# A one-core hybrid layer with routed experts: small loads on ScalarE's queue, tables in strips, later bias loads, unread products

## The reference, cut to what matters

```python
h = h + hybrid_mixer(rms_norm(h, norm1_gain), w_in, ...)   # ends in concat([h_m, h_g]) @ w_out
hn = rms_norm(h, norm2_gain)
logits = hn @ w_router + b_router                           # 512 x 32
top_logit, top_idx = lax.top_k(logits, 4); gate = softmax(top_logit)
# for each expert e, the tokens that chose it, in blocks:
hb = xb @ w_up[e] + b_up[e]                                  # 1024 -> 2048
act = min(glu, 7) * sigmoid(1.702 * min(glu, 7)) * (clip(lin, -7, 7) + 1)
y  += (act @ w_down[e] + b_down[e]) * gate
out = rms_norm(h + y, final_gain)
```

## Time and profile before

| what | value |
|---|---|
| median of three runs | 1299.21 us |
| profiled execution | 1301.6 us, its span 1298.9 us |
| TensorE busy | 1131.2 us, 87% of the span |
| chain that ended last | DMA 58%, PE 30%, SPq 6%, DVE 3% |
| HBM traffic | 447.43 MB read, 25.04 MB written, 364 GB/s over the span |
| mixer and first tiles | up to some 273 us |
| routing | some 273 to 301 us |
| experts | some 301 to 1257 us |
| sums and final norm | to 1298.9 us |

### The profile page before, as it was taken

One profiled execution on the slowest core, in us unless ns is written; L12 is line 12 of the kernel. 1 busy time (PEld: TensorE's weight loads), 2 busy tenths in 40 slices (PEclk: granted clock), 3 DMA queues, 4 the chain that ended last, 5 costly groups with the idle time before them and its releaser, 6 DMA issues.

```text
span 1298.9 us, 28681 instructions
## 1 busy us (share of the span) xinstructions
PE 1131.2 (87%) x11031; PEld 519.3 (40%) x11032; DVE 496.7 (38%) x1245; ACT 201.7 (16%) x293; POOL 217.6 (17%) x384
## 2 busy tenths in 40 slices
PE   8999999989989998989989898989797989797750
PEld 4445554534434443434444333434343434343320
DVE  1393453564423432423343332323233323232317
ACT  2104321111111111111111111111111111111101
POOL 1000112001212221212221111212121212121112
PEclk9999999989979999989999999999899999999995
DMA  9308307668999999999999999999999999999997
GB/s 352 119 33 280 109 1 300 242 234 341 419 422 405 412 425 427 425 426 427 424 426 426 423 425 425 424 425 424 422 426 426 424 427 422 422 426 424 425 419 278
DMA packets 67945, 472.84 MB, mean 364 GB/s; under 512 B 9072, under 2 KB 27052, under 8 KB 42704
## 3 DMA queue, kind: packets, MB, share of 16 engines
q1 hardware_dynamic: 57928, 447.29, 83.4%
q0 software_dynamic: 7776, 20.46, 4.1%
q10 hardware_dynamic: 2216, 4.75, 1.0%
HBM read 447.43 MB, written 25.04 MB: 364 GB/s over the span
## 4 chain that ended last, share of the span: by engine, by line
DMA 58%; PE 30%; SPq 6%; DVE 3%; issue 3%; ACT 0%; POOL 0%; POOLq 0%; DVEq 0%; ACTq 0%
DMA W<-in_w_up_dram 55%; PE B L1271 11%; PE B L1569 8%; PE B L1423 3%; PE B L1586 3%; PE B L1302 2%; SPq L314 2%; SPq L319 1%; SPq L397 1%; DMA W<-in_b_router_dram 1%; SPq L399 1%; DMA hres<-misc,idx_s 1%; DVE W L1233 1%; DMA W<-in_w_in_dram 0%; DVE W L1234 0%
## 5 line engine op out<-in xcount | busy, mean ns | idle before, releaser
L1569 PE MATMUL B<-W,misc 128*32 128x512 f32 x4992 | 593.4, 622 | 114.7 <-DMA W<-in_w_up_dram 90.4
L1569 PEld LDWEIGHTS B<-W,misc 128*32 128x32 f32 x4992 | 186.0, 113 | 469.9 <-issue 463.8
L1586 PE MATMUL B<-W,misc 128*32 128x256 f32 x4992 | 286.8, 380 | 1.1 <-DVE misc L1178 0.9
L1586 PEld LDWEIGHTS B<-W,misc 128*32 128x32 f32 x4992 | 191.3, 111 | 119.0 <-issue 50.0
L1158 DVE TENSOR_TENSOR misc<-B,misc 128x512 f32<-128x512 f32 x78 | 54.0, 692 | 409.0 <-PE B L1569 408.3
L696 ACT ACTIVATE misc<-misc 128x256 f32<-128x256 f32 x78 | 32.5, 416 | 821.1 <-DVE misc L1162 821.1
L1271 PE MATMUL B<-W 128*128 128x512 f32 x320 | 140.2, 593 | 0.0
L513 POOL COPY idx_g<-idx_tab 128x1 uint32 (+1 forms) x77 | 14.3, 185 | 583.3 <-DVE misc L1192 559.2
L696 ACT ACT_TABLE_LOAD x78 | 100.1, 1283 | 9.3 <-DVE idx_tab L1141 7.9
L525 POOL DMA_INDIRECT yrow<-misc,idx_s x75 | 75.1, 1002 | 135.0 <-DVE misc L1180 135.0
L1271 PEld LDWEIGHTS B<-W 128*128 128x128 f32 x320 | 59.6, 190 | 69.1 <-issue 69.1
(11 more groups left out here) (294 smaller groups left out, 514.9 us busy)
## 6 DMA issues: line engine op xcount, KB each, us to landing
W<-in_w_up_dram SPq DMA_DIRECT2D x128, 2048.0 KB, 13.3
W<-in_w_down_dram SPq DMA_DIRECT2D x64, 2048.0 KB, 9.8
W<-in_w_in_dram SPq DMA_DIRECT2D x5, 2048.0 KB, 19.8
yrow<-W SPq DMA_DIRECT2D x1, 8192.0 KB, 40.9
W<-yrow SPq DMA_DIRECT2D x4, 2048.0 KB, 19.9
W<-in_x_dram SPq DMA_DIRECT2D x8, 512.0 KB, 6.8
W<-in_w_out_dram SPq DMA_DIRECT2D x1, 4096.0 KB, 15.7
W<-in_w_in_dram SPq DMA_DIRECT2D x2, 1024.0 KB, 7.0
```

The lines of the kernel that those rows point to most:

```text
L1569: ins = mm(B[0][BT * j:BT * (j + 1), :].rearrange("p (g h c) -> p g h c", g=2, h=2), xT[:, BT * k:BT * (k + 1)], up(par)[:, k, :, :, P * j ...
L1586: ins = mm(B[5][BT * j:BT * (j + 1), 0:QC], aT[:, BT * q:BT * (q + 1)], down(par)[:, q, QC * j:QC * (j + 1)], start=(q == 0), stop=(q == N ...
```

## The change

Four edits. (1) The four small loads are issued by ScalarE, on its queue, after `squares_gating` of tile 3 and ahead of `squares_h(0)`, under the same three waits, in the order `wr`, `rb`, two gain rows. SP keeps the three waits. TensorE's wait for them moves from `router_turn(0)` to `router_strips(0)`. (2) `table` writes its 16 products to four strips of 32 partitions in turn; the small tables and the spreading matrices get 128 partitions, and `spread_table` sums over 128 rows instead of 32. (3) The up-bias row is loaded ahead of piece 3 instead of piece 1, the down-bias row behind piece 5 instead of ahead of piece 4, each with its wait. (4) `busy(n)` makes n products of 128 rows and 128 columns that nothing reads; ten of them stand ahead of four waits in the routing stage.

```diff
 # SP
-            for n in range(2):
-                sp.dma_start(n2row[n], norm2_gain[...].broadcast_to([P, 512])).then_inc(s_n2row, 16)
-            sp.dma_start(wr, w_router[0].rearrange("(k p) n -> p k n", p=P)).then_inc(s_n2row, 16)
-            sp.dma_start(rb, b_router.broadcast_to([P, NE])).then_inc(s_n2row, 16)
...
-                        if n == 1:
+                        if n == 3:
                             sp.wait_ge(m_z, done)
                             load_bias_up(sp, par, e)
-                        if n == 4:
-                            sp.wait_ge(m_ys, done)
-                            load_bias_dn(sp, par, e)
                         if n >= AHEAD:
                             sp.wait_ge(s_w[par][n - AHEAD], 16 * i + 16)
                         load_piece(sp, par, n, e)
+                    sp.wait_ge(m_ys, done)
+                    load_bias_dn(sp, par, e)
 # ScalarE, between squares_gating(3) and squares_h(0)
+            act.wait_ge(s_p, NT * H)
+            act.wait_ge(s_hm, NT)
+            act.wait_ge(s_hgr, NT)
+            act.dma_start(wr, ...).then_inc(s_n2row, 16)
+            act.dma_start(rb, ...).then_inc(s_n2row, 16)
+            for n in range(2):
+                act.dma_start(n2row[n], ...).then_inc(s_n2row, 16)
 # VectorE
-                V.tensor_copy(spread16, ident[0:BT, 0:BT]...)
-                V.tensor_copy(spread, ident[0:BT, 0:BT]...)
+                V.tensor_copy(spread16, fold32.unsqueeze(1).broadcast_to([P, H, BT]))
+                V.tensor_copy(spread, fold32.unsqueeze(1).broadcast_to([P, H, BT]))
-            V.tensor_copy(tok_s, B[5][0:BT, 0:NBMAX])
+            V.tensor_copy(tok_s, B[5][:, 0:NBMAX])
-                V.tensor_copy(gate_s, B[1][0:BT, 0:NBMAX])
+                V.tensor_copy(gate_s, B[1][:, 0:NBMAX])
 # TensorE
 router_turn:
-                else:
-                    pe.wait_ge(s_n2row, 64)
 router_strips:
+                if c == 0:
+                    pe.wait_ge(s_n2row, 64)
 table:
-                    ins = mm(B[bank][0:BT, 0:NBMAX], U[:, a, :], G[:, a, :], start=(a == 0), stop=(a == NT * TOPK - 1))
+                    s = a % 4
+                    ins = mm(B[bank][BT * s:BT * (s + 1), 0:NBMAX], U[:, a, :], G[:, a, :], start=(a < 4), stop=(a >= 12))
...
+            def busy(n):
+                for _ in range(n):
+                    mm(B[4][:, 0:128], ident[:], wr[:, 0:4, :], start=True, stop=True)
             pe.wait_ge(s_pick, 1)
             pick_rows(0, range(NT - 1))
+            busy(2)
             pe.wait_ge(s_mk, NT)
...
+            busy(3)
             pe.wait_ge(s_pick, 2)
             pick_rows(0, range(NT - 1, NT)).then_inc(s_picked, 1)
+            busy(1)
             late_rows()
+            busy(4)
             place_ranks()
```

More of the change, by code:

```diff
@@ L226, in hybrid_layer @@
         lo16, hi16 = r(8).bitcast(f16), r(8).bitcast(f16)
-        tok_s, gate_s = r(48).bitcast(f16)[0:BT, :], r(96)[0:BT, :]
-        spread16 = r(64).bitcast(f16)[0:BT, :].rearrange("p (j t) -> p j t", j=H)
-        spread = r(128)[0:BT, :].rearrange("p (j t) -> p j t", j=H)
+        tok_s, gate_s = r(48).bitcast(f16), r(96)
+        spread16 = r(64).bitcast(f16).rearrange("p (j t) -> p j t", j=H)
+        spread = r(128).rearrange("p (j t) -> p j t", j=H)
         G32 = R[:, 14360:15896].rearrange("p (a g) -> p a g", a=16)
@@ L367, in _ @@
             sp.wait_ge(s_hgr, NT)
-            for n in range(2):
-                sp.dma_start(n2row[n], norm2_gain[:, 512 * n:512 * (n + 1)].broadcast_to([P, 512])).then_inc(s_n2row, 16)
-            sp.dma_start(wr, w_router[0].rearrange("(k p) n -> p k n", p=P)).then_inc(s_n2row, 16)
-            sp.dma_start(rb, b_router.broadcast_to([P, NE])).then_inc(s_n2row, 16)
             first(1, 1)
@@ L406, in _ @@
                             load_bias_up(sp, par, e)
-                        if n == 4:
-                            sp.wait_ge(m_ys, done)
-                            sp.nop(nofuse=True)
-                            load_bias_dn(sp, par, e)
                         if n >= AHEAD:
@@ L413, in _ @@
                         load_piece(sp, par, n, e)
+                    sp.wait_ge(m_ys, done)
+                    sp.nop(nofuse=True)
+                    load_bias_dn(sp, par, e)
             done = sp.value_load(base_tab[0:1, NE - 1:NE], min_val=NE - 1, max_val=NBMAX - 2)
@@ L683, in _ @@
                             (gelu_vg, 2), (squares_vg, 2), (squares_gating, 0), (gelu_u, 2), (squares_gating, 1),
-                            (gelu_vg, 3), (squares_vg, 3), (squares_gating, 2), (gelu_u, 3), (squares_gating, 3),
-                            (squares_h, 0), (squares_h, 1), (squares_h, 2), (squares_h, 3)):
+                            (gelu_vg, 3), (squares_vg, 3), (squares_gating, 2), (gelu_u, 3), (squares_gating, 3)):
                 step(c)
+            act.wait_ge(s_p, NT * H)
+            act.wait_ge(s_hm, NT)
+            act.wait_ge(s_hgr, NT)
+            act.dma_start(wr, w_router[0].rearrange("(k p) n -> p k n", p=P)).then_inc(s_n2row, 16)
+            act.dma_start(rb, b_router.broadcast_to([P, NE])).then_inc(s_n2row, 16)
+            for n in range(2):
+                act.dma_start(n2row[n], norm2_gain[:, 512 * n:512 * (n + 1)].broadcast_to([P, 512])).then_inc(s_n2row, 16)
+            for c in range(NT):
+                squares_h(c)
             act.wait_ge(s_v8, 1)
@@ L1009, in routing_constants @@
                 V.tensor_copy(tokm, tokm_i)
-                V.tensor_copy(spread16, ident[0:BT, 0:BT].unsqueeze(1).broadcast_to([BT, H, BT]))
-                V.tensor_copy(spread, ident[0:BT, 0:BT].unsqueeze(1).broadcast_to([BT, H, BT]))
                 V.tensor_scalar(part_i[:, 1:2], part_i[:, 0:1], 5, None, ALU.logical_shift_right)
@@ L1020, in routing_constants @@
                 link(V.tensor_scalar(expb, ones, partf[:, 0:1], None, ALU.mult))
-                V.tensor_reduce(fold32, ident[:].rearrange("p (a n) -> p n a", a=4), AXX, ALU.add)
+                link(V.tensor_reduce(fold32, ident[:].rearrange("p (a n) -> p n a", a=4), AXX, ALU.add))
+                V.tensor_copy(spread16, fold32.unsqueeze(1).broadcast_to([P, H, BT]))
+                V.tensor_copy(spread, fold32.unsqueeze(1).broadcast_to([P, H, BT]))
             for c in range(NT):
@@ L1129, in _ @@
             dve.wait_ge(s_tabs, 1)
-            V.tensor_copy(tok_s, B[5][0:BT, 0:NBMAX]).then_inc(s_small_tab, 1)
+            V.tensor_copy(tok_s, B[5][:, 0:NBMAX]).then_inc(s_small_tab, 1)
             dve.wait_ge(s_order, 1)
@@ L1146, in gates_done @@
                 dve.wait_ge(s_tabs, 2)
-                V.tensor_copy(gate_s, B[1][0:BT, 0:NBMAX]).then_inc(s_small_tab, 1)
+                V.tensor_copy(gate_s, B[1][:, 0:NBMAX]).then_inc(s_small_tab, 1)
                 dve.wait_ge(s_spread, 2)
```

## The result

The changed kernel is slower: 1309.91 us, median of ten runs (1307.26 to 1312.62), against 1301.78 us for the kernel before (1298.92 to 1304.88) beside it, a ratio of 1.0069 (95% interval 1.0058 to 1.0081). The forecast was +6.4 us on the median, to 1305.6, within 1296 to 1312; measured is +8.1 between the medians. The kernel before itself came out 2.6 us above the median that the forecast started from, so the difference is the fairer measure.

A forecast was written before the change was run, and what follows sets the result against it. Bound before some 301 us by occupied weight buffers and the TensorE-VectorE chain, then by transfer bytes over bandwidth. Edits 1, 4 and 3 and the last expert: +10.8 - 2.0 - 2.5 + 0.1 = +6.4 on 1299.2, so 1305.6 us, range 1296 to 1312.

The forecast's parts named there:

- The landing: Small loads ahead of the router's strips: land at 237.2 us, between 228 and 240; strips +9.1 us.
- the loss of clock behind it: TensorE behind the strips: clock falls after standing 13.6 us, +1.7 us (0 to 3.4).
- The first rival: Router's strips: small loads land before 223.6, so the kernel is faster, -8.9 to 1290.3 us; chance 0.15.
- The third: Small loads' queue: engine takes many small packets in one turn, landing at 228.1; -2.7, 1296.5 us; chance 0.10.
- The single report of an end in 5.8 us: DMA queues: the want of reports in the earlier profile was held against many small packets passing in one turn.
- the pace of rows 5: Small loads' queue: earlier profile's 101 packets in 5.8 us; 1408 would take 81 us, about 460 pass up to 235.
- the bound that VectorE sets: Routing stage: VectorE's L1121 ends at 292.03, L1124 began at 294.09, so the gain ends at 2.06 us: -2.0.
- VectorE hides the tables: Routing stage's tables: strips may save up to 2 us of table 2, but VectorE hides it: 0 (-0.5 to +0.2).
- VectorE's wait for the late down-bias row: Expert stage, before an expert's second block: 0, at worst some 0.5 us in an expert of several blocks.
- 0.1 for the last expert: End of the expert stage: the later down-bias row adds 0 to 0.5 us in the last expert, taken as +0.1.
- The second rival: Routing and expert stages: edits 3 and 4 give nothing; +10.8 to +11.5, 1310 to 1311 us; chance 0.15.

The follow-up runs named there:

- b_hold: Changed kernel, but SP waits for the four small loads before issuing (1,1), (1,4) and (1,5); 1294.11 us, 0.9946 of the kernel before.
- b_weights_on_sp: Changed kernel with only the router weights back on SP's queue, ahead of (1,1); 1296.04 us, 0.9963 of the kernel before.
- b_small_first: Changed kernel with plain tables and the four small loads on SP's queue ahead of (0,0) and (0,1); 1292.11 us, 0.9941 of the kernel before.
- c_changed_fill: Changed kernel with 14 more unread products in the table stretch, nothing else; 1308.66 us, 1.0048 of the kernel before.
- c_strips_no_fill: As b_small_first, but with tables in strips and no added products in the table waits; 1295.46 us, 0.9951 of the kernel before.
- a_tables_plain: Changed kernel with the tables made in one strip of 32 partitions again; 1308.65 us, 1.0061 of the kernel before.
- a_bias_back: Changed kernel with the bias rows loaded ahead of pieces 1 and 4 again; 1313.44 us, 1.0090 of the kernel before.

## Why the prediction was right, and where it was off

**Edit 1** was sized well and by the right mechanism. The landing was foreseen at 237.2 and came at 238.44, 14.3 us after TensorE stopped, where 13.6 were forecast. Counted from the first residual the strips came 9.38 us later than before (forecast 9.1); the loss of clock behind it was 1.78 us (238.48 to 243.73 for the strips and what follows up to the next transposes, before 228.06 to 231.53) against 1.7. The first rival (early loads, 1290.3 us) fell in the measurement, and b_hold shows the condition under which it would have been true. The third (many small packets in one turn) fell with 11 to 11 and 2 to 2 packets in 0.27 us. By the rule of the Trainium skill that goes with it, DMA: Bandwidth & Descriptors, section Queues, rings and completion order, an engine drains a packet of several descriptors from one ring before it turns; the trace does not agree. The single report of an end in 5.8 us, on which the step rested, excludes only turns as long as a transfer's share of an engine; the short windows after exclude turns of two.

Two sizes inside the step were wrong and did no harm. It let some 460 of the small packets pass up to 235 us, at the pace of rows 5, where 790 passed: in 219 to 224 us the pace was 29 packets per us and not 17. And it gave the four issues some 0.4 us each, where they took from 207.48 to 218.72. Both are without effect because the landing hangs on the moment when q1 runs dry, and that was taken from the earlier trace rows. That step was sound; with fewer small packets the pace decides, as in b_weights_on_sp.

**Edit 4** shortened its stretch as forecast, to the bound that VectorE sets: -2.05 us against -2.0. But how much of it the products did is less sure. Taken out of the changed kernel they give back 0.44 us of the stretch, out of b_small_first 1.39, and neither shows in the time. What the step left out is that a fall avoided in one place can come in the next.

**Edit 2** is the term that failed. The step said that VectorE hides the tables, so 0. It does hide them. But the time taken out of the two tables, 0.48 us (0.84 to 0.36) and 1.96 us (2.83 to 0.87), became idle time of TensorE, which grew from 1.10 to 4.44 us in its two pieces (the rest of the growth is TensorE's earlier arrival), and the clock fell behind it: +1.57 us in the profile. c_changed_fill and c_strips_no_fill show that filling these pieces keeps the clock up. All seven kernels with strips and nothing to fill them had the fall, and one of the four with plain tables. The plain tables were no cure where the clock fell in any case (a_tables_plain); so the +1.57 belongs to the tables together with the place in time at which they stand, and I had counted the clock only for the stretch before them. With +1.57 the sum would have been +8.0, near the measured +8.1; so close a match is partly luck, as the spans differ by 9.6 and the medians by 8.1.

**Edit 3** was -2.7 us by a_bias_back, -2.11 from the profile and -2.1 by the landing of the last piece, forecast -2.5 with 0.1 for the last expert. The step had VectorE's wait for the late down-bias row at 0 to 0.5 us. It waits 12.9 us in all for that row and 73.7 for the up-bias row, but TensorE isn't held by it, so the step's cost was right and its wait was not.

The second rival (edits 3 and 4 worth nothing) gave 1310 to 1311, near the measured 1309.91, but as a difference it gave +10.8 to +11.5, and +8.1 is nearer the forecast's +6.4. Edit 3 speaks against it. For edit 4 it isn't refuted: its gain is in the traces and not in the times.

## What to carry to other kernels

Before a load is moved to another queue to free it from what stands ahead of it, count its packets and look at the packet size of the queue beside it: here each packet of 128 bytes waited for one of 16 KB, so that the last 682 of 1472 passed only as the other queue ran dry. Order within one queue did better: small loads first, large ones behind, 4.8 us gained where the second queue had lost 11. Where TensorE's clock matters, a product group made shorter in front of a wait can lengthen what follows; fill the wait, or leave the work in it.

## What the runs showed of the hardware that I had not expected

Sharing between two queues was exact, 146 to 146 packets, with sizes 128 to 1 apart. ScalarE's sequencer was held for 9.30 us in all by issuing the two gain rows (209.42 to 218.72), as SP's had been for 9.94 us at one issue. The same two issues took 1.12 us in b_weights_on_sp, where the 1024 packets of the weights didn't stand ahead of them; so it looks like a queue with limited room, whose size the runs don't show. It cost nothing only because ScalarE's next work came at 219.77. And the clock's fall came in the table stretch, where the kernel before had none, in eight of the twelve other kernels, the changed one among them; in ten of the twelve the unread products had taken the earlier fall out of the routing stage. In seven the up-projection behind it took 8.43 to 10.01 us instead of 7.07, in the eighth table 2 took it. It came in neither of the two with the waits filled, nor in the two with plain tables and the small loads first.
